# One accumulation region per slab: three matmuls of 256 columns in place of one of 512 and one of 256

## The reference

```python
proj = h @ w_in                      # mixer, 37 slabs of 128 output channels
x = x + gate_a * rms_norm(y, g)      # y = mix @ w_out, 16 slabs
y = jnp.square(jax.nn.relu(h @ w_up)) @ w_down   # 128 slabs
# third layer: h @ w_in (32 slabs), y @ w_glu (16), y @ w_out (16)
# fourth: h @ w_kv (33), h @ w_in (32), o @ w_out (16)
```

## Time and profile before

| what | us |
|---|---|
| median of 3 runs | 3213.59 |
| the profiled execution | 3216.8 |
| its span | 3214.8 |
| PE busy | 3090.5 |
| PEld busy | 2693.4 |
| DVE busy | 2517.6 |
| ACT busy | 1561.1 |
| mean granted clock | 0.987 of full speed |

### The profile page before, as it was taken

How to read it: one execution, slowest core, us unless ns; L and a number is a source line. 1 busy time by engine, 2 the same in 40 slices (tenths; PEclk the granted TensorE clock), 3 DMA queues, 4 the chain that set the end, 5 groups by cost and what they waited for, 6 DMA issues and landing times.

```text
span 3214.8 us, 49733 instructions
## 1 busy us (share of the span) xinstructions
PE 3090.5 (96%) x20432; PEld 2693.4 (84%) x20432; DVE 2517.6 (78%) x3179; ACT 1561.1 (49%) x2338; POOL 0.2 (0%) x4
## 2 busy tenths in 40 slices
PE   4899999999999999999999999999998899999998
PEld 3787778888888888888888888888887788888887
DVE  7997999788988888777987666797669677656765
ACT  2455654444444566666544444446443456334454
POOL 0000000000000000000000000000000000000000
PEclk7999999999999999999999999999999999999999
DMA  9777869988889646654687666885654553654453
GB/s 409 306 295 303 316 233 347 344 335 334 338 332 340 253 160 217 222 219 166 238 314 282 234 207 232 296 288 189 227 172 168 182 188 139 223 184 157 145 190 110
DMA packets 136978, 790.27 MB, mean 246 GB/s; under 512 B 20081, under 2 KB 38897, under 8 KB 46001
## 3 DMA queue, kind: packets, MB, share of 16 engines
q1 hardware_dynamic: 119714, 769.33, 64.8%
q10 hardware_dynamic: 17040, 17.76, 1.6%
HBM read 769.28 MB, written 17.76 MB: 245 GB/s over the span
## 4 chain that ended last, share of the span: by engine, by line
PE 51%; DVE 3%; issue 1%; ACT 1%; ACTq 0%; DVEq 0%
PE bk L410 51%; DVE wl L1563 1%; DVE pr L1563 1%; DVE Hst L1563 0%; DVE ss L1563 0%; PE bk L414 0%; DVE tmp L1563 0%; DVE X L1563 0%; DVE z L1563 0%; DVE z L1571 0%; ACT wh L900 0%; DVE qa L1571 0%; DVE p L1563 0%; ACT ln L900 0%; DVE hg L1571 0%
## 5 line engine op out<-in xcount | busy, mean ns | idle before, releaser
L1563 DVE TENSOR_TENSOR wl<-raw,wh 128x2048 fp32r<-128x2048 f32 (+1 forms) x484 | 1097.2, 2267 | 230.5 <-ACT wh L900 230.2
L410 PE MATMUL bk<-HX,wh 128*128 128x512 f32 x4592 | 1113.7, 395 | 1.2 <-issue 1.1
L410 PEld LDWEIGHTS bk<-HX,wh 128*128 128x128 f32 x4592 | 843.5, 188 | 173.4 <-issue 2.1
L900 ACT ACTIVATE wh<-raw 128x2048 fp32r<-128x2048 f32 x479 | 913.7, 1908 | 49.1 <-DMA raw<-in_w_out 24.0
L410 PEld LDWEIGHTS bk<-HX,wl 128*128 128x128 f32 x4592 | 572.0, 188 | 30.7 <-DVE wl L1563 7.8
L410 PE MATMUL bk<-HX,wl 128*128 128x256 f32 x4592 | 579.3, 278 | 4.1 <-DVE wl L1563 4.1
L410 PE MATMUL bk<-hb,wh 128*128 128x512 f32 (+1 forms) x2080 | 491.8, 389 | 0.4 <-ACT hb L900 0.3
L1571 DVE SCALAR_TENSOR_TENSOR raw<-raw,cb 128x2048 f32<-128x2048 f32 x192 | 437.3, 2284 | 13.6 <-DMA raw<-in_w_ada 13.5
L410 PEld LDWEIGHTS bk<-hb,wh 128*128 128x128 f32 x2080 | 377.1, 188 | 74.5 <-ACT hb L900 0.7
L410 PEld LDWEIGHTS bk<-hb,wl 128*128 128x128 f32 x2048 | 255.5, 188 | 10.5
L410 PE MATMUL bk<-hb,wl 128*128 128x256 f32 x2048 | 258.0, 278 | 0.0
(11 more groups left out here) (308 smaller groups left out, 2705.5 us busy)
## 6 DMA issues: line engine op xcount, KB each, us to landing
raw<-in_w_ada SPq DMA_DIRECT2D x192, 1024.0 KB, 6.3
raw<-in_w_up SPq DMA_DIRECT2D x128, 1024.0 KB, 5.4
raw<-in_w_down SPq DMA_DIRECT2D x128, 1024.0 KB, 5.0
raw<-in_w_in SPq DMA_DIRECT2D x68, 1024.0 KB, 5.4
raw<-in_kv_w SPq DMA_DIRECT2D x33, 1024.0 KB, 4.8
raw<-in_w_out SPq DMA_DIRECT2D x32, 1024.0 KB, 4.8
raw<-in_s_w_in SPq DMA_DIRECT2D x32, 1024.0 KB, 5.0
raw<-in_fox_w_in SPq DMA_DIRECT2D x32, 1024.0 KB, 4.7
```

The costliest lines, as they stand in the source:

```text
L410: return e.matmul(o_, l_, r_, start=start, stop=stop, skip_group_check=True)
L900: return e.activation(o_, i_, f, **kw)
L1563: return e.tensor_tensor(o_, a_, b_, op)
```

## The change

Every slab sums into columns 0 to 255 by three matmuls of 256 columns per block. One operation of one engine then takes the bank: ACT in most stages (`copied`, or the GLU's tanh straight from the bank), DVE for the down projection, for the gate slab and where it already did (`BY_VECTOR`). `half`, `joined`, `s_half`, `s_yt` and `s_gt2` are gone. Since both engines count on `s_ev`, the taking engine waits for the slab before where the other engine took that one (`bank_of`).

```diff
-                one = j - 15 in TURNS
                 for q, k in enumerate(order):
-                    if one:
-                        for part in range(2):
-                            mm(bank[:, 0:T], WH[w][:, k, :], x(k)[:, part, :], q == 0 and part == 0, False)
-                        continue
                     if first:
                         first(k)
-                    mm(bank[:, :], WH[w][:, k, :], x(k).rearrange("p a t -> p (a t)"), q == 0, False)
+                    for part in range(2):
+                        mm(bank[:, 0:T], WH[w][:, k, :], x(k)[:, part, :], q == 0 and part == 0, False)
...
-            def half(j, dst, rows=slice(0, P), scale=1.0):
+            def bank_of(j):
                 e.wait_ge(s_slab, j + 1)
-                act(dst, BK[BANK_OF[j]][rows, T:2 * T], ACT.Copy, scale=scale).then_inc(s_half, 1)
+                if j and j - 1 in BY_VECTOR:
+                    e.wait_ge(s_ev, j)
+                return BK[BANK_OF[j]][:, 0:T]
+            def copied(j, dst, scale=1.0):
+                act(dst, bank_of(j), ACT.Copy, scale=scale).then_inc(s_ev, 1)
...
-            def joined(j, dst, scale=1.0):
-                e.wait_ge(s_half, HALF_AT[j])
-                ps = BK[BANK_OF[j]][:, 0:T]
-                if scale == 1.0:
-                    tt(dst, ps, dst, ALU.add).then_inc(s_ev, 1)
...
-            def down_joined(l, j, n):
+            def down_added(l, j, n):
...
-                joined(down_slab(l, j, n), yt if j == 3 else y)
-                if j:
-                    e.wait_ge(s_ev, down_slab(l, j, n) + 1)
-                    tt(yt if j == 3 else y, y, yt, ALU.add).then_inc(s_yt, 1)
+                ps = bank_of(down_slab(l, j, n))
+                if j == 0:
+                    e.tensor_copy(y, ps).then_inc(s_ev, 1)
+                else:
+                    e.wait_ge(s_ev, down_slab(l, j - 1, n) + 1)
+                    tt(yt if j == 3 else y, ps, y, ALU.add).then_inc(s_ev, 1)
...
-                half(J_GLU + n, ZF[n % 2][:, :])
-            def glu_tanh(n):
-                e.wait_ge(s_ev, J_GLU + n + 1)
-                act(ZF[n % 2][:, :], ZF[n % 2][:, :], ACT.Tanh, scale=0.5, bias=NB[:, n:n + 1]).then_inc(s_gt2, 1)
+                act(ZF[n % 2][:, :], bank_of(J_GLU + n), ACT.Tanh, scale=0.5, bias=NB[:, n:n + 1]).then_inc(s_ev, 1)
```

More of the change, by code:

```diff
@@ L148 @@
     HI_AT.append(_n)
[L149 to L152, removed]
+TAKEN = {_j for _t in TURNS[:-1] for _j in range(_t + 16, _t + 16 + SIDE)}
+BY_VECTOR = (TAKEN | {AT_G}
+             | {down_slab(_l, _p, _n) for _l in range(2) for _p in range(4) for _n in range(16)})
 PLACE_OF = [-1 if j in DIRECT else HI_AT[j] % 2 for j in range(N_SLABS)]
@@ L464, in ramp @@
                             e.wait_ge(s_hf, k + 1)
-                            c0 = 0 if k < 8 else T
-                            last = mm(banks[r][:, c0:c0 + T], RAMPW[r][:, k, :], HF[:, k, :], k % 8 == 0, k % 8 == 7)
+                            last = mm(banks[r][:, 0:T], RAMPW[r][:, k, :], HF[:, k, :], k == 0, k == KT - 1)
                 last.then_inc(s_slab, RAMP)
@@ L668, in first_out @@
                         mixed(k)
-                        mm(bank[:, :], WH[w][:, k, :], mixer_out(k).rearrange("p a t -> p (a t)"), k == 8, False)
+                        for part_ in range(2):
+                            mm(bank[:, 0:T], WH[w][:, k, :], mixer_out(k)[:, part_, :], k == 8 and part_ == 0, False)
                     e.wait_ge(s_free, FREE_AT[POS[j]])
@@ L961, in y_parts @@
                 last = n == 15 and i not in (1, 3)
-                if n < 15 and i in (1, 3):
-                    e.wait_ge(s_yt, 47 * (i // 2) + 32 + n + 1)
-                elif not last:
+                if not last:
                     e.wait_ge(s_ev, TURNS[i] + n + 1)
@@ L1039, in mixer_half @@
                         e.wait_ge(s_vt, c - 1)
-                    half(j, TV[c % 2][:, :])
+                    copied(j, TV[c % 2][:, :])
                 elif kind in ("q", "k"):
@@ L1045, in mixer_half @@
                         e.wait_ge(s_qk, c - 1)
-                    half(j, CV[s][:, 3:3 + T])
+                    copied(j, CV[s][:, 3:3 + T])
                 elif kind == "os":
@@ L1049, in mixer_half @@
                         e.wait_ge(s_hg, 4 * l + (i - 4) // 2 + 1)
-                    half(j, OS[i % 4][:, :])
+                    copied(j, OS[i % 4][:, :])
                 else:
-                    half(j, (KA if kind == "ka" else QA)[:, i, :])
+                    copied(j, (KA if kind == "ka" else QA)[:, i, :])
             def out_gate(l, v):
@@ L1225, in mixer_tasks, with up_copied @@
                         out_gate(l, 5)
[L1228 to L1233, removed]
+            def up_copied(l, j, n):
+                if up_slab(l, j, n) in TAKEN:
+                    return
+                e.wait_ge(s_ul, 64 * l + 16 * j + n - 1)
+                copied(up_slab(l, j, n), UR[n % 2][:, :])
             def up_high(l, j, n):
@@ L1410, in third @@
                     if n:
-                        half(J_Z + n - 1, Z[:, n - 1, :])
+                        copied(J_Z + n - 1, Z[:, n - 1, :])
                     next_high(J_Z + n)
@@ L1460, in kv_half @@
                         e.wait_ge(s_kt, v - 1)
-                    half(J_KV + n, FV[v % 2][:, :])
+                    copied(J_KV + n, FV[v % 2][:, :])
             def f_gates():
@@ L1671, in y_times_x @@
                     return
[L1672 to L1675, removed]
+                e.wait_ge(s_ev, TURNS[i] + n + 1)
                 if n >= 4:
@@ L1805, in gates_scanned, with mixer_taken @@
                 tt(gt, gt, gf, ALU.add).then_inc(s_gd, 1)
-            def mixer_joined(l, n):
-                kind, i = SLABS[n]
-                if kind == "gate":
+            def mixer_taken(l, n):
+                if SLABS[n][0] == "gate":
                     gate_taken(l)
[L1811 to L1821, removed]
+                elif l and 0 < n < SIDE:
+                    shifted(n, TV[0][:, :])
             def conv(l, i, s):
```

179 lines of the change are left out of this document (62 added, 117 removed).

## The result

Four executions of the changed kernel took 3231.71 to 3241.88 us, median 3235.81 us, against 3213.64 us before (four executions, 3213.51 to 3213.86). The ratio is 1.0071, 95% interval 1.0059 to 1.0083: slower by 0.7%, 22 us, where +13 to +15 us was forecast. The executions of the changed kernel also lie 10 us apart, those before 0.35 us. The profiled execution is the slowest of the four, 3241.88 us with a span of 3240.1.

The account below looks back on a forecast made before the run. The prediction took PE, busy 96% of the span, as the bound: +33 us for narrower matmuls and -18 us of waits made +15, 3228.6 us, shaded by 2 to 3227. Its own range was 3218 to 3245, over the cases 3184 to 3264.

Parts of the forecast that it names:

- The sign and the two terms: Whole kernel: narrower matmuls cost PE +33 us, fewer waits held by DVE and ACT give -18 us, so slower.
- Two spacings: Runs of 256-column matmuls keep 113 or 118 ns from entry: 5.45 or 5.66 us per slab, against 5.516 before.
- Two thirds slow: Share of the 473 slabs at the slow spacing, from four of six seen: mean 5.59 us, +33 us in all.
- Neither side has slack: At 256 columns a weight load, estimated at 107 ns, takes as long as the columns take to stream.
- the slow rival: 118 ns in every slab, with weight loads as the place: +66 - 14, 3266 us; chance 0.20, nearly slow included.
- First output projection: DVE sets the pace from 357 to 445 us; without the join 5.72 for 6.14 us per slab, -5 us.
- Hst: PE's 8.7 us wait at the end of the third layer's `z` slabs: about -3.5 us, 5 us remaining.
- ta, mx, wh, go: PE's 15.4 us of waits in the mixers and at the output projections' starts: half comes back, -7 us.
- The added waits: `bank_of` makes ACT and DVE wait for each other: 0 us, at most 1 us at each of 12 places.
- DVE's work: Over the whole run DVE is busy some 170 us less, from 345 joins of 0.42 us and 96 additions.

Follow-up runs that it names:

- split512: The kernel before, halves and joins kept, with each 512-column matmul issued as two of 256: 3251.74 us, ratio 1.012.
- relief512: The changed kernel with the 512-column matmul put back, its low half taken by nobody, so one product is left out: 3196.49 us, ratio 0.9948.
- wide_probe: The changed kernel with one to six extra 512-column matmuls ahead of every second slab: 3408.95 us in a single run.
- fill_probe: The changed kernel with one extra matmul of 0 to 256 columns ahead of each slab, eight slabs per width in turn: 3297.23 us in a single run.
- low192: The changed kernel with the second of three matmuls per block cut from 256 to 192 columns: 3216.74 us in a single run.

## Why the prediction was right

*The sign and the two terms.* Right, and measured apart: +39 us for the matmuls (split512) where +33 stood, -16 us for the relief (relief512) where -18 stood. That both sizes came so close is in part luck, since errors inside each term cancel, as the next points show.

*Two spacings.* Right: 5.44 and 5.65 us per slab, kept through long stretches, the first MLP +17 us as worked out for the slow one.

*Two thirds slow.* Mis-sized. Four of six slabs was a thin sample; the profiled execution has 85% slow. By the prediction's own prices, 0.14 us dearer and 0.07 cheaper, 84% slow as in split512's trace would be 473 x 0.106 = +50 us, not +33. That execution measured +41 and the median +39. So the share was too low and the price, charged to every slab, too high. The first output projection paid nothing (98.2 us in both kernels), and in the first mixer 26 slabs paid 1.2 us together; where the rest of the 10 us went was not traced. The prediction took 2 us off for dearer slabs before. The table of wide_probe suggests why few slabs are fast: of the three phases that 512s cycle through only one gives 113 ns, and fill_probe adds that each width from 16 to 224 leads to 118. It also means that a number of one execution is partly a draw. I gave the spread between cases, and none to executions of one kernel; it is 10 us.

*Neither side has slack.* I had this under the slow rival, as the weight load being the place. low192 and fill_probe show it of the weight load, in slabs at 118 ns: fewer columns gain next to nothing. No run shortened the load, so for the columns it is an estimate: a 512 takes 229 ns, half of it 114.5. The Trainium skill ("TensorE: Matmul & The Clock Gate", section "LDWEIGHTS (loading the stationary operand)") puts a load at its columns over 1.2, an estimated 107 ns for 128; the trace agrees within 6 to 11 ns per matmul, measured as spacing, and PEld's rows with their 188 ns include the overlap. By the gaps of isolated matmuls in the section "Back-to-back issue gap" of that page, two 256s cost 2.5 ns more than one 512, estimated +19 us in all; split512 measured +39, 5.2 ns. The measurement decides.

*First output projection.* -5 us was forecast, -6.1 measured, DVE's 0.46 us per slab (5.68 for 6.14). The DMA loads allowed it, at a share of 0.94. As relief it was under-sized: relief512 gains 8.1 us here (90.1 for 98.2). In the changed kernel PE is busy for 92.09 of the stage's 92.10 us, so its slabs of 5.65 us took 2.0 of that back.

*Hst.* 5 us of wait were forecast to remain, 5.7 did. The way there was only half as described: DVE's lag behind ACT was to be worked off, 2.9 us of it. The last pair of `wh` and `wl` before the state chain, after, against the earlier trace rows:

```profile
2484.98 1.91 ACT L892 ACTIVATE wh<-raw 128x2048 fp32r<-128x2048 f32 x1
2488.77 2.28 DVE L1532 TENSOR_TENSOR wl<-raw,wh 128x2048 fp32r<-128x2048 f32 x1
```

`wh` ends at 2486.89, so the lag is still 1.9 us. The slabs of DVE are 5.27 us there (2488.77 - 2483.50) against 5.65 of PE, so it shrinks by 0.4 us a slab. That is 1 us of the 3.0 that the wait lost, and the missing join in the chain behind it is 0.3 more, as forecast; the rest was not traced.

*ta, mx, wh, go.* -7 us was forecast; 15.4 became 11.7, -3.7. ta and wh did not move, though DVE had less to do. In those places the join was not what the chain waited for; what is, no run told. The 3 us too much here and the 3 us too little in the first output projection cancel in the -18.

*The added waits.* 0 was right as far as it shows: no PE wait for a bank appears, and the MLP's length is slabs x 5.65 us.

*DVE's work.* "Some 170 us less" was forecast and 177 measured; the 345 joins and 96 additions named with it would be 441 x 0.42 = 185 us.

Open: what starts a stretch in one phase or the other after small matmuls or a wait, and why executions differ in it.

## What to carry to other kernels

When a matmul is cut into two with the same weights, count the weight loads. Here a matmul with a full load of 128 columns took 113 ns with 16 columns as with 256, and one of 512 columns 229 ns, so at 256 columns PE had lost its slack. The price is read from the spacing of starts, not from mean durations. Relief of another engine is worth at most what PE loses to it, stage by stage: of 31.6 us of such waits 16 came back. Here a change of 31 slabs kept 8 of the 16 us and left out the 39. Before trusting a median of such a kernel, see whether its executions spread.

## What the runs showed of the hardware that was not expected

Runs of 256-column matmuls with a load each go at 113 or at 118 ns and stay there for up to 359 groups of 16; a filler of 16 to 224 columns ended at 118, and extra 512-column matmuls stepped through the phases with a period of three, but for a single one behind kind a. One 512-column matmul more or less at a stretch's start changed 120 slabs by 0.21 us each: 683.1 against 708.5 us for the same work but for that matmul. A matmul with a full load cost 113 ns with 16 columns as with 256. In two traces a fast stretch ended right behind a stop of PE inside a slab.
